# A gated-delta branch whose odd tile is multiplied first, with its norms moved and two memsets on GpSimd

## The chip, the cores and the metric

The kernel runs on one core of a Trainium2 chip. The metric is the device time of one execution in microseconds (us); a kernel's time is the median of several. Five engines work side by side and meet through semaphores: TensorE (PE, with PEld for its weight loads) multiplies, VectorE (DVE) and ScalarE (ACT) work element by element and can read TensorE's accumulator banks (`ps`), GpSimd (POOL) works element by element in on-chip memory, and SyncE (SP) issues the transfers (DMA). Each engine takes its own instructions strictly in order. An instruction that waits holds up all that stand behind it in its engine's queue.

## The reference, cut to what matters

The reference is a stack: a first block with two layers (three branches side by side in each: gated delta, latent attention, RWKV-7) and then a second block. The change lies in the gated-delta branch of the first block, so it is run twice. All is float32, one sequence of 1024 tokens with 1024 features.

```python
def gdn_branch(cols, conv_w, a_log, dt_bias, norm_g):   # cols = rms_norm(x) @ w_in, by columns
    qkv = jnp.concatenate([cols['gdn_q'], cols['gdn_k'], cols['gdn_v']], axis=-1)  # 384 + 384 + 384
    qkv = jax.nn.silu(centred_depthwise_conv(qkv, conv_w))                         # 5 taps in time
    q, k, v = jnp.split(qkv, [GDN_QK_W, 2 * GDN_QK_W], axis=-1)
    q = l2_normalize(q.reshape(b, l, GDN_HEADS, GDN_DK)) * (GDN_DK ** -0.5)
    k = l2_normalize(k.reshape(b, l, GDN_HEADS, GDN_DK))
    ...
    g = -jnp.exp(a_log) * jax.nn.softplus(a + dt_bias)
    beta = jax.nn.sigmoid(bt)
    o = gated_delta_chunked(...)                         # the next stage, in both directions
    o = rms_norm(bidir_merge(o), norm_g)
```

## The kernel before, in words

The stage is called `gdn_front` (lines 1488 to 1871 of the kernel before). It computes q, k and v up to the recurrence: 1152 columns, cut into nine tiles of 128. Feature-major, each tile is a matrix of 128 columns by 1024 tokens: tiles 0 to 2 are q, 3 to 5 are k, 6 to 8 are v. `hT` is the normed input, transposed.

For each tile n: multiply (TensorE), put the result into a padded buffer (`x_pad_g`, called `xp`), five taps of the convolution on VectorE in two halves of the tokens (`taps(n, b)`: one TENSOR_SCALAR and four SCALAR_TENSOR_TENSOR), and `silu` of each half on ScalarE into `gq`. The first six tiles (`NORMED`) are normed too: squares on GpSimd (`sq_g`), their sums by a matmul with a block matrix (`square_sums(n)`), `Ln` and `Exp` on ScalarE (`inverse_norm(n)`, into `rs_g`), and a product on VectorE (`normed(n)`). ScalarE has to load a table ahead of a function of another kind (ACT_TABLE_LOAD).

Eight of the nine tiles are multiplied in four pairs. A pair is a product of 2 by 2 blocks, done with seven block products in place of eight: P1 to P7, each four matmuls. Its inputs are the combinations T1 to T4 of blocks of `hT` (`combos_g`, once for the stage) and the sums S1 to S4 of blocks of the weights (`sums_g`, once for each pair). P1, P6, P7 and P4 add up one after the other in one bank of `ps`, and after each of the first three ScalarE copies the bank (`keep(1..3, j)` into `kept_g`), so each next one waits for that copy. P2 has a bank of its own; P5 and P3 add up in another. Three of the four result blocks are put together by VectorE (`block_of`: c11, c22, c12), the fourth (c21) is copied by ScalarE after P4 (`last_block`). The ninth tile is multiplied whole, in two halves of eight matmuls (`whole(b)`).

Pair j is tiles 2j and 2j+1, and the whole tile is number 8, last. The order on every engine is the one in which the code is written, engine by engine; no scheduler changes it. A buffer of `xp`, `acc_g`, `sq_g`, `rs_g` holds two tiles, chosen by n % 2. Weights of tiles 0 to 2 have been loaded by the stage ahead; SP loads the rest as their slots come free. The next stage (`gdn_chunk`) begins behind a barrier of all engines.

Of the kernel before, what the change touches and what calls it, by code (L numbers as in the profile page):

```python
# [25 lines left out]
ALU = mybir.AluOpType  # L26
# [110 lines left out]
def build(nc, io, values):  # L137
    with ExitStack() as ctx:
# [97 lines left out]
        for L in range(DEPTH):  # L236
# [1251 lines left out]
            with ExitStack() as st:  # L1488
# [11 lines left out]
                with ExitStack() as st2, nc.Block() as block:  # L1500
# [13 lines left out]
                    NP, WHOLE = 4, 8  # L1514
# [11 lines left out]
                    def left(j, r, k):  # L1526
                        return slot(2 * j + r)[:, 4 * k:4 * k + 4, :]
# [10 lines left out]
                    def inside(r, b):  # L1538
                        return xp[:, r, 2 + b * 512:2 + (b + 1) * 512]

                    def ready(n, b):
                        if n == WHOLE:
                            return ACT[f"whole_{b}"]
                        j, r = n // 2, n % 2
                        return ACT[f"c21_{j}"] if (r, b) == (1, 0) else VEC[f"c{r + 1}{b + 1}_{j}"]

                    @block.sync
                    def _(sp):
                        def columns(n):
                            sp.dma_start(slot(n), w_rows(w_in[:, COL_GDN + n * P:COL_GDN + (n + 1) * P])).then_inc(*DMA(f"w{n}"))  # L1550

                        columns(3)
                        sp.dma_start(tm_ab[:, :, :], tm_hbm[:, 0:2 * G2].rearrange("(t p) n -> p t n", p=P)).then_inc(*DMA("ab"))
                        for j in range(2, NP):
                            sp.wait_ge(*PE[f"P4_{j - 2}"])
                            sp.wait_ge(*VEC[f"S4_{j - 2}"])
                            columns(2 * j)
                            columns(2 * j + 1)
                        sp.wait_ge(*PE[f"P4_{NP - 2}"])
                        sp.wait_ge(*VEC[f"S4_{NP - 2}"])  # L1560
                        columns(WHOLE)

                    @block.tensor
                    def _(pe):
# [5 lines left out]
                        def first(j):  # L1570
                            if j >= 1:
                                pe.wait_ge(*DMA[f"w{2 * j}"] if j > 1 else DMA["w3"])
                            if j >= 2:
                                pe.wait_ge(*ACT[f"c21_{j - 2}"])
                            product("P1", j, chain_bank(j), left(j, 0, 0), right(0, 0))

                        def second(j):
                            if j:
                                pe.wait_ge(*VEC[f"c11_{j - 1}"])
                            product("P2", j, B_BANK, left(j, 0, 1), right(1, 0))  # L1580
# [20 lines left out]
                        def fifth(j):  # L1601
                            if j:
                                pe.wait_ge(*VEC[f"c12_{j - 1}"])
                            product("P5", j, D_BANK, sm[:, j % 2, 0], T[:, 0])

                        def fourth(j):
                            if j == 0:
                                pe.wait_ge(*VEC["T4"])
                            if j > 1:
                                pe.wait_ge(*DMA[f"w{2 * j + 1}"])  # L1610
                            pe.wait_ge(*ACT[f"s3_{j}"])
                            product("P4", j, chain_bank(j), left(j, 1, 1), T[:, 3], start=False)

                        def whole(b):
                            if b == 0:
                                pe.wait_ge(*DMA[f"w{WHOLE}"])
                                pe.wait_ge(*ACT[f"c21_{NP - 2}"])
                            else:
                                pe.wait_ge(*VEC[f"c11_{NP - 1}"])
                            for k in range(KD):  # L1620
                                q = pe.matmul(ps[:, (chain_bank(NP), B_BANK)[b], :], lhsT=slot(WHOLE)[:, k, :], rhs=hT[:, k, P + b * 512:P + (b + 1) * 512],
                                              start=(k == 0), stop=(k == KD - 1))
                            q.then_inc(*PE(f"whole_{b}"))
# [18 lines left out]

                        first(0)
                        second(0)
                        sixth(0)
                        fifth(0)
                        seventh(0)
                        gate_sums()
                        fourth(0)
                        for j in range(1, NP):  # L1650
                            first(j)
                            third(j - 1)
                            sixth(j)
                            second(j)
                            seventh(j)
                            fifth(j)
                            fourth(j)
                            square_sums(2 * j - 2)
                            square_sums(2 * j - 1)
                        whole(0)  # L1660
                        third(NP - 1)
                        whole(1)

                    @block.scalar
                    def _(act):
# [6 lines left out]
                        def last_block(j):  # L1672
                            act.wait_ge(*PE[f"P4_{j}"])
                            if j:
                                act.wait_ge(*VEC[f"tap{2 * j - 1}_1_{LAST}"])
                            act.copy(inside(1, 0), ps[:, chain_bank(j), :]).then_inc(*ACT(f"c21_{j}"))

                        def whole(b):
                            act.wait_ge(*PE[f"whole_{b}"])
                            act.wait_ge(*VEC[f"tap{WHOLE - 2}_1_{LAST}"])  # L1680
                            act.copy(inside(0, b), ps[:, (chain_bank(NP), B_BANK)[b], :]).then_inc(*ACT(f"whole_{b}"))
# [34 lines left out]

                        keep(1, 0)
                        gates()
                        keep(2, 0)
                        keep(3, 0)  # L1720
                        last_block(0)
                        gate_ends()
                        for j in range(1, NP):
                            keep(1, j)
                            silu(2 * j - 2, 0)
                            silu(2 * j - 1, 0)
                            silu(2 * j - 1, 1)
                            keep(2, j)
                            silu(2 * j - 2, 1)
                            keep(3, j)  # L1730
                            last_block(j)
                            inverse_norm(2 * j - 2)
                            inverse_norm(2 * j - 1)
                        silu(2 * NP - 2, 0)
                        silu(2 * NP - 1, 0)
                        silu(2 * NP - 1, 1)
                        silu(2 * NP - 2, 1)
                        whole(0)
                        whole(1)
                        silu(WHOLE, 0)  # L1740
                        silu(WHOLE, 1)

                    @block.vector
                    def _(vec):
# [10 lines left out]
                        def sums_of_left(j, which):  # L1755
                            a11, a12, a21, a22 = (left(j, r, k) for r, k in ((0, 0), (0, 1), (1, 0), (1, 1)))
                            if which == 0:
                                for n in (2 * j, 2 * j + 1):
                                    if n > 2:
                                        vec.wait_ge(*DMA[f"w{n}"])  # L1760
# [11 lines left out]
                        def block_of(j, r, b):  # L1772
# [3 lines left out]
                            vec.tensor_tensor(inside(r, b), kept[:, n - 1, :], ps[:, bank, :], ALU.add).then_inc(*VEC(f"c{r + 1}{b + 1}_{j}"))  # L1776
# [20 lines left out]
                        def cleared():  # L1797
                            vec.memset(G[:, :, :, :], 0.0).then_inc(*VEC("G"))
                            vec.memset(S[:, :, :, :], 0.0).then_inc(*VEC("S"))

# [18 lines left out]

                        combos_open()  # L1820
                        sums_of_left(0, 0)
                        sums_of_left(0, 1)
                        gates()
                        combos_close()
                        gate_rates()
                        block_of(0, 0, 0)
                        cleared()
                        taps(0, 0)
# [3 lines left out]
                        taps(1, 0)  # L1832
                        block_of(0, 0, 1)
                        taps(1, 1)
                        for j in range(1, NP):
                            taps(2 * j - 2, 1)
                            block_of(j, 0, 0)
                            taps(2 * j, 0)
                            if j == 1:
                                vec.wait_ge(*ACT["beta"])  # L1840
                                vec.wait_ge(*ACT["ends1"])
                                vec.tensor_tensor(kdw[:, :, :], kdw[:, :, :], gb[:, :, 1, :], ALU.mult).then_inc(*VEC("kdw"))
                            else:
                                normed(2 * j - 4)
                                normed(2 * j - 3)
# [4 lines left out]
                            taps(2 * j + 1, 0)  # L1850
                            block_of(j, 0, 1)
                            taps(2 * j + 1, 1)
                        taps(2 * NP - 2, 1)
                        normed(NORMED - 2)
                        normed(NORMED - 1)
                        taps(WHOLE, 0)
                        taps(WHOLE, 1)

                    @block.gpsimd
                    def _(pool):  # L1860
                        pool.memset(Y64[:, :, :, :], 0.0).then_inc(*POOL("Y64"))
                        for n in range(NORMED):
# [2548 lines left out]
```

## Time and profile before

| what | us |
|---|---|
| median of 3 runs (3723.2 to 3729.97) | 3729.53 |
| the profiled execution, its own time | 3734.25 |
| its span, first to last instruction | 3732.2 |
| `gdn_front`, first layer: 391.98 to 528.62 | 136.64 |
| `gdn_front`, second layer: 1518.43 to 1655.06 | 136.63 |
| PE busy in the first of them | 123.58 |
| DVE busy in it | 106.75 |
| ACT busy in it | 61.01 |
| POOL busy in it | 18.37 |

Times in the trace count from the start of the span. A row of the timeline gives start, duration, engine, line, operation, output<-inputs and count; in brackets the idle time of the engine ahead of it and what ended it. Instructions of one line that follow each other are merged, and the end of a product of matmuls is modelled: its 3.60 us overlap the next one by 0.17. Each float32 matmul shows as two. In the second layer the buffers are the same with `_again` behind their names.

### The profile page before, as it was taken

The page shows a single profiled execution, that of the slowest core. Times are in us where ns is not written, and L with a number is a line of the kernel's source. Part 1 is how long each engine was busy: PE and PEld are TensorE (multiplying, and loading weights), DVE is VectorE, ACT ScalarE, POOL GpSimd, SP SyncE. Part 2 cuts the span into 40 slices and gives each one's busy share as a digit, 9 for nine tenths or more (in the row PEclk, how much of TensorE's full clock was granted, in tenths as well). Part 3 has the DMA queues.
Part 4 walks back from the last instruction along what each step waited for, and adds up shares of the span by engine and source line. Part 5 has one row for each costly group of instructions (what it writes and reads, how often), then busy time and mean ns, then how long its engine had stood idle before and what let it go on. Part 6 is the DMA issues. An engine that isn't in the chain of part 4 may idle for free. (4 is left out here: it accounts for less than half of the span.)

```text
span 3732.2 us, 65872 instructions
## 1 busy us (share of the span) xinstructions
PE 3451.9 (92%) x27864; PEld 2104.2 (56%) x27864; DVE 2325.3 (62%) x4083; ACT 1221.8 (33%) x2143; POOL 290.5 (8%) x233
## 2 busy tenths in 40 slices
PE   7888879989999879988989988999999997999999
PEld 4367436666644467436766644666666664444444
DVE  3586778876653487678876653467766667433453
ACT  3353354535431254354534432122212121321002
POOL 0010100000000011100000000222222220000000
PEclk9899999999999999999999998999999998999999
DMA  4334212220053333312220042111111102213221
GB/s 164 104 92 131 67 34 85 81 101 12 13 187 113 99 90 111 93 34 85 80 103 12 10 156 82 35 41 45 46 41 46 40 24 87 86 42 112 90 96 45
DMA packets 302164, 281.51 MB, mean 75 GB/s; under 512 B 18208, under 2 KB 274592, under 8 KB 301872
## 3 DMA queue, kind: packets, MB, share of 16 engines
q1 hardware_dynamic: 301872, 277.30, 23.1%
q8 instruction: 222, 3.64, 0.4%
q14 instruction: 70, 0.57, 0.0%
HBM read 203.93 MB, written 73.33 MB: 74 GB/s over the span
## 5 line engine op out<-in xcount | busy, mean ns | idle before, releaser
L3716 DVE SCALAR_TENSOR_TENSOR cv<-glu,params,cv 128x1024 f32<-128x1024 f32 x240 | 361.0, 1504 | 6.4
L413 PE MATMUL ps<-hT,w_cols 128*128 128x512 f32 x448 | 198.9, 602 | 1.6 <-PEq L160 1.6
L4012 PE MATMUL ps<-hT,wr 128*128 128x512 f32 x360 | 161.7, 592 | 0.0
L413 PEld LDWEIGHTS ps<-hT,w_cols 128*128 128x128 f32 x448 | 85.2, 192 | 111.3 <-issue 111.2
L3692 POOL TENSOR_TENSOR Sp<-Sp,Rp 128x520 f32<-128x520 f32 (+1 forms) x56 | 88.5, 1581 | 566.2 <-DVE W L3733 566.2
L3475 PE MATMUL ps<-hT,w_f 128*128 128x347 f32 x384 | 116.3, 462 | 6.1 <-DMA w_f<-in_w_in 6.1
L3490 PE MATMUL ps<-w_i,hT 128*128 128x128 f32 x1024 | 120.7, 277 | 0.0
L3490 PEld LDWEIGHTS ps<-w_i,hT 128*128 128x128 f32 x1024 | 116.1, 192 | 2.2 <-issue 1.6
L4012 PEld LDWEIGHTS ps<-hT,wr 128*128 128x128 f32 x360 | 68.4, 190 | 86.1 <-issue 86.1
L3329 PE MATMUL ps<-w_out_again,mT_again 128*128 128x512 f32 x256 | 115.8, 612 | 0.0
L3475 PE MATMUL ps<-hT,w_glu_a 128*128 128x347 f32 x384 | 114.2, 456 | 0.4 <-ACT sgb L3656 0.4
L3482 PE MATMUL ps<-hT,w_g 128*128 128x512 f32 x256 | 114.1, 599 | 0.0
L3329 PE MATMUL ps<-w_out,mT 128*128 128x512 f32 x256 | 113.9, 604 | 0.0
L3475 PE MATMUL ps<-hT,w_glu_b 128*128 128x347 f32 x384 | 113.4, 454 | 0.0
L3482 PE MATMUL ps<-hT,w_q 128*128 128x512 f32 x256 | 111.2, 592 | 0.0
L4012 PE MATMUL ps<-combos_even,sums_of_w 128*128 128x512 f32 x240 | 107.9, 592 | 0.0
L3475 PEld LDWEIGHTS ps<-hT,w_f 128*128 128x128 f32 x384 | 72.9, 192 | 45.8 <-DMA w_f<-in_w_in 6.5
L1972 PE MATMUL ps<-fw_again,fh_again 128*128 128x384 f32 x256 | 91.2, 519 | 6.7 <-DVE AT_again L2368 3.5
L4098 ACT COPY kept_sums<-ps 128x512 f32<-128x512 f32 x46 | 27.0, 586 | 210.5 <-PE ps L4012 210.3
L3695 POOL TENSOR_TENSOR Rp<-Rp 128x520 f32<-128x520 f32 (+1 forms) x56 | 94.3, 1683 | 4.4
L2836 PE MATMUL ps<-kT_again,qT_again 96*128 96x512 f32 x192 | 92.5, 605 | 1.8 <-PEq L160 1.8
L2836 PE MATMUL ps<-kT,qT 96*128 96x512 f32 x192 | 92.5, 605 | 1.8 <-PEq L160 1.8
(975 smaller groups left out, 7350.9 us busy)
## 6 DMA issues: line engine op xcount, KB each, us to landing
w_cols<-in_w_in SPq DMA_DIRECT2D x30, 512.0 KB, 4.2
wr<-in_w_in SPq DMA_DIRECT2D x24, 512.0 KB, 5.2
hT_hbm<-hT SPq DMA_DIRECT2D x2, 4096.0 KB, 14.0
hT<-hT_hbm SPq DMA_DIRECT2D x2, 4096.0 KB, 15.9
fh<-hT_hbm SPq DMA_DIRECT2D x16, 512.0 KB, 4.7
fh_again<-hT_hbm SPq DMA_DIRECT2D x16, 512.0 KB, 4.6
x<-in_x SPq DMA_DIRECT2D x8, 512.0 KB, 9.0
ahead<-kb_hbm SPq DMA_DIRECT2D x16, 256.0 KB, 3.3
```

The costliest lines, as they stand in the source:

```text
L413: q = pe.matmul(ps[:, proj_bank(n, b), :], lhsT=wc[:, n % 3, k, :], rhs=hT[:, k, P + b * 512:P + (b + 1) * 512], start=(k == 0), stop=(k = ...
L1972: q = pe.matmul(ps[:, WB + n % 2, 0:FILL], lhsT=fh[:, n % 2, k, :], rhs=fw[:, k, :], start=(k == 0), stop=(k == KD - 1))
L2836: q = pe.matmul(ps[:, SCORES + 2 * (j % 2) + b, :], lhsT=qT[:, h, t * P:(t + 1) * P], rhs=kT[:, h, b * 512:(b + 1) * 512], start=True, sto ...
L3329: q = pe.matmul(ps[:, sum_bank(t, b), :], lhsT=mT[:, t % 2, k, :], rhs=wo[:, k, 512 * b:512 * (b + 1)], start=(k == 0), stop=(k == KD - 1))
L3475: q = pe.matmul(ps[:, BANK_X + b, 0:LONG], lhsT=wt[n][:, k, :], rhs=hT[:, k, T0 + b * LONG:T0 + (b + 1) * LONG], start=(k == 0), stop=(k = ...
L3482: q = pe.matmul(ps[:, bank + b, :], lhsT=wt[n][:, k, :], rhs=hT[:, k, P + b * 512:P + (b + 1) * 512], start=(k == 0), stop=(k == KD - 1))
L3490: q = pe.matmul(ps[:, BANK_X + b, (t % 3) * P:(t % 3 + 1) * P], lhsT=hT[:, k, t * P:(t + 1) * P], rhs=wt["i"][:, k, :], start=(k == 0), st ...
L3692: pool.tensor_tensor(S4[:, :, 0, :], S4[:, :, 0, :], R4[:, :, 1, (1 << k) - 1:1 << k].broadcast_to([P, n, 1 << k]), ALU.mult).then_inc(*PO ...
L3695: pool.tensor_tensor(R4[:, :, 1, :], R4[:, :, 1, :], R4[:, :, 0, (1 << k) - 1:1 << k].broadcast_to([P, n, 1 << k]), ALU.mult).then_inc(*PO ...
L3716: vec.scalar_tensor_tensor(out=cv[:, h % 2, :], in0=src, scalar=w, in1=cv[:, h % 2, :], op0=ALU.mult, op1=ALU.add).then_inc(*VEC(f"tap{h}_ ...
L4012: q = pe.matmul(ps[:, to, :], lhsT=a[:, k, :], rhs=b[:, k, :], start=(start and k == 0), stop=(k == 3), skip_group_check=True)
L4098: act.copy(sn[:, n // 2, :], ps[:, bank(j, "a"), :]).then_inc(*ACT(f"s{n}_{j}"))
```

## The change

The whole tile becomes tile 0 and is multiplied first, into the banks of P2 and P5; pair j is now tiles 2j+1 and 2j+2. Pair 0 runs P1, P6, P2, P7, P5, P4, where it ran P1, P2, P6, P5, P7, P4. The sums of squares of tile 2j-1 stand ahead of P4 of pair j, those of tile 2j behind it. `normed(2j-2)` and `normed(2j-1)` are done in pair j, where `normed(2j-4)` and `normed(2j-3)` were. The gates' first part stands at the head of VectorE's queue, and the memsets of `G` and `S` go from VectorE to GpSimd.

The diff, without three hunks that only renumber tiles:

```diff
-NP, WHOLE = 4, 8
+NP, WHOLE = 4, 0
...
 def left(j, r, k):
-    return slot(2 * j + r)[:, 4 * k:4 * k + 4, :]
+    return slot(2 * j + 1 + r)[:, 4 * k:4 * k + 4, :]
...
 def sum_bank(n, b):
...
-def inside(r, b):
-    return xp[:, r, 2 + b * 512:2 + (b + 1) * 512]
+def inside(n, b):
+    return xp[:, n % 2, 2 + b * 512:2 + (b + 1) * 512]
...
 def ready(n, b):
...
-    j, r = n // 2, n % 2
+    j, r = (n - 1) // 2, (n - 1) % 2
...
+    sp.wait_ge(*PE["whole_1"])
+    columns(4)
     for j in range(2, NP):
...
-        columns(2 * j)
...
-    sp.wait_ge(*PE[f"P4_{NP - 2}"])
-    sp.wait_ge(*VEC[f"S4_{NP - 2}"])
-    columns(WHOLE)
+        columns(2 * j + 2)
...
     def second(j):
...
+        else:
+            pe.wait_ge(*ACT["whole_0"])
...
     def fifth(j):
...
+        else:
+            pe.wait_ge(*ACT["whole_1"])
...
     def fourth(j):
...
-        if j > 1:
-            pe.wait_ge(*DMA[f"w{2 * j + 1}"])
+        if j:
+            pe.wait_ge(*DMA[f"w{2 * j + 2}"])
...
     def whole(b):
-        if b == 0:
-            pe.wait_ge(*DMA[f"w{WHOLE}"])
-            pe.wait_ge(*ACT[f"c21_{NP - 2}"])
-        else:
-            pe.wait_ge(*VEC[f"c11_{NP - 1}"])
         for k in range(KD):
-            q = pe.matmul(ps[:, (chain_bank(NP), B_BANK)[b], :], lhsT=slot(WHOLE)[:, k, :], rhs=hT[:, k, P + b * 512:P + (b + 1) * 512],
+            q = pe.matmul(ps[:, (B_BANK, D_BANK)[b], :], lhsT=slot(WHOLE)[:, k, :], rhs=hT[:, k, P + b * 512:P + (b + 1) * 512],
...
             pe.matmul(ps[:, sum_bank(n, b), :], lhsT=blk, rhs=sq[:, n % 2, half(b)], start=True,
                       stop=True).then_inc(*PE(f"sumsq{n}_{b}"))
 
+    whole(0)
+    whole(1)
     first(0)
+    sixth(0)
     second(0)
-    sixth(0)
-    fifth(0)
     seventh(0)
     gate_sums()
+    fifth(0)
     fourth(0)
+    square_sums(0)
...
         second(j)
         seventh(j)
         fifth(j)
+        square_sums(2 * j - 1)
         fourth(j)
-        square_sums(2 * j - 2)
-        square_sums(2 * j - 1)
-    whole(0)
+        if 2 * j < NORMED:
+            square_sums(2 * j)
     third(NP - 1)
-    whole(1)
...
     def last_block(j):
...
-        if j:
-            act.wait_ge(*VEC[f"tap{2 * j - 1}_1_{LAST}"])
-        act.copy(inside(1, 0), ps[:, chain_bank(j), :]).then_inc(*ACT(f"c21_{j}"))
+        act.wait_ge(*VEC[f"tap{2 * j}_1_{LAST}"])
+        act.copy(inside(2 * j + 2, 0), ps[:, chain_bank(j), :]).then_inc(*ACT(f"c21_{j}"))
...
     def whole(b):
...
-        act.wait_ge(*VEC[f"tap{WHOLE - 2}_1_{LAST}"])
-        act.copy(inside(0, b), ps[:, (chain_bank(NP), B_BANK)[b], :]).then_inc(*ACT(f"whole_{b}"))
+        act.copy(inside(WHOLE, b), ps[:, (B_BANK, D_BANK)[b], :]).then_inc(*ACT(f"whole_{b}"))
...
                 q = act.activation(to, whole, FN.Exp)
             q.then_inc(*ACT(f"ends{e}"))
 
+    whole(0)
+    whole(1)
     keep(1, 0)
     gates()
     keep(2, 0)
+    silu(WHOLE, 0)
+    silu(WHOLE, 1)
     keep(3, 0)
+    gate_ends()
     last_block(0)
-    gate_ends()
+    inverse_norm(0)
     for j in range(1, NP):
         keep(1, j)
-        silu(2 * j - 2, 0)
         silu(2 * j - 1, 0)
+        silu(2 * j, 0)
+        keep(2, j)
+        silu(2 * j, 1)
         silu(2 * j - 1, 1)
-        keep(2, j)
-        silu(2 * j - 2, 1)
         keep(3, j)
         last_block(j)
-        inverse_norm(2 * j - 2)
         inverse_norm(2 * j - 1)
-    silu(2 * NP - 2, 0)
-    silu(2 * NP - 1, 0)
-    silu(2 * NP - 1, 1)
-    silu(2 * NP - 2, 1)
-    whole(0)
-    whole(1)
-    silu(WHOLE, 0)
-    silu(WHOLE, 1)
+        if 2 * j < NORMED:
+            inverse_norm(2 * j)
+    for n, b in ((2 * NP - 1, 0), (2 * NP, 0), (2 * NP, 1), (2 * NP - 1, 1)):
+        silu(n, b)
...
-
-    def cleared():
-        vec.memset(G[:, :, :, :], 0.0).then_inc(*VEC("G"))
-        vec.memset(S[:, :, :, :], 0.0).then_inc(*VEC("S"))
...
         vec.wait_ge(*ACT[f"rs{n}"])
         vec.tensor_tensor(gq[:, n, :], gq[:, n, :], rs[:, n % 2, :], ALU.mult).then_inc(*VEC(f"normed{n}"))
 
+    gates()
     combos_open()
     sums_of_left(0, 0)
+    taps(WHOLE, 0)
     sums_of_left(0, 1)
-    gates()
     combos_close()
+    taps(WHOLE, 1)
     gate_rates()
     block_of(0, 0, 0)
-    cleared()
-    taps(0, 0)
+    taps(1, 0)
     sums_of_left(1, 0)
     sums_of_left(1, 1)
     block_of(0, 1, 1)
-    taps(1, 0)
+    taps(2, 0)
+    taps(2, 1)
+    vec.wait_ge(*ACT["beta"])
+    vec.wait_ge(*ACT["ends1"])
+    vec.tensor_tensor(kdw[:, :, :], kdw[:, :, :], gb[:, :, 1, :], ALU.mult).then_inc(*VEC("kdw"))
     block_of(0, 0, 1)
     taps(1, 1)
     for j in range(1, NP):
-        taps(2 * j - 2, 1)
+        normed(2 * j - 2)
         block_of(j, 0, 0)
-        taps(2 * j, 0)
-        if j == 1:
-            vec.wait_ge(*ACT["beta"])
-            vec.wait_ge(*ACT["ends1"])
-            vec.tensor_tensor(kdw[:, :, :], kdw[:, :, :], gb[:, :, 1, :], ALU.mult).then_inc(*VEC("kdw"))
-        else:
-            normed(2 * j - 4)
-            normed(2 * j - 3)
+        taps(2 * j + 1, 0)
         if j + 1 < NP:
             sums_of_left(j + 1, 0)
             sums_of_left(j + 1, 1)
         block_of(j, 1, 1)
-        taps(2 * j + 1, 0)
+        normed(2 * j - 1)
+        taps(2 * j + 2, 0)
+        taps(2 * j + 2, 1)
         block_of(j, 0, 1)
         taps(2 * j + 1, 1)
-    taps(2 * NP - 2, 1)
-    normed(NORMED - 2)
-    normed(NORMED - 1)
-    taps(WHOLE, 0)
-    taps(WHOLE, 1)
 
 @block.gpsimd
 def _(pool):
     pool.memset(Y64[:, :, :, :], 0.0).then_inc(*POOL("Y64"))
+    pool.memset(G[:, :, :, :], 0.0).then_inc(*POOL("G"))
+    pool.memset(S[:, :, :, :], 0.0).then_inc(*POOL("S"))
```

TensorE, between P4 of pair 1 and P6 of pair 2. `combos_g,w_cols` is P4 or P7, `sq_g` the sums of squares, `hT,w_cols` P1 or P2, `hT,sums_g` P3, `combos_g,sums_g` P6 or P5. Before:

```order
L1567 MATMUL ps<-combos_g,sums_g 128x512 x4
L1567 MATMUL ps<-combos_g,w_cols 128x512 x4
L1640 MATMUL ps<-sq_g,consts 128x512 x4
L1567 MATMUL ps<-hT,w_cols 128x512 x4
L1567 MATMUL ps<-hT,sums_g 128x512 x4
L1567 MATMUL ps<-combos_g,sums_g 128x512 x4
```

and after:

```order
L1566 MATMUL ps<-combos_g,sums_g 128x512 x4
L1638 MATMUL ps<-sq_g,consts 128x512 x2
L1566 MATMUL ps<-combos_g,w_cols 128x512 x4
L1638 MATMUL ps<-sq_g,consts 128x512 x2
L1566 MATMUL ps<-hT,w_cols 128x512 x4
L1566 MATMUL ps<-hT,sums_g 128x512 x4
L1566 MATMUL ps<-combos_g,sums_g 128x512 x4
```

Two of the four matmuls of the squares' sums went ahead of P4.

ScalarE at the same place, from the third copy of a pair to the first of the next (`rs_g` is `inverse_norm`), after the change:

```order
L1670 COPY kept_g<-ps 128x512
L1675 COPY x_pad_g<-ps 128x512
L1691 ACT_TABLE_LOAD
L1691 ACTIVATE rs_g<-ps,consts 128x512 x2
L1693 ACT_TABLE_LOAD
L1693 ACTIVATE rs_g<-rs_g 128x1024
L1691 ACT_TABLE_LOAD
L1691 ACTIVATE rs_g<-ps,consts 128x512 x2
L1693 ACT_TABLE_LOAD
L1693 ACTIVATE rs_g<-rs_g 128x1024
L1670 COPY kept_g<-ps 128x512
```

It is the same row for row as before, with other line numbers; only the tiles of the two norms are others.

VectorE at the end of the stage (`x_pad_g<-kept_g` is `block_of`, `gq<-gq,rs_g` is `normed`, 510 and 514 are the first and second half of a tile's taps). Before:

```order
L1776 TENSOR_TENSOR x_pad_g<-kept_g,ps 128x512
L1810 TENSOR_SCALAR acc_g<-x_pad_g,params 128x514
L1813 SCALAR_TENSOR_TENSOR acc_g<-x_pad_g,params,acc_g 128x514 x4
L1810 TENSOR_SCALAR acc_g<-x_pad_g,params 128x514
L1813 SCALAR_TENSOR_TENSOR acc_g<-x_pad_g,params,acc_g 128x514 x4
L1818 TENSOR_TENSOR gq<-gq,rs_g 128x1024 x2
L1810 TENSOR_SCALAR acc_g<-x_pad_g,params 128x510
L1813 SCALAR_TENSOR_TENSOR acc_g<-x_pad_g,params,acc_g 128x510 x4
L1810 TENSOR_SCALAR acc_g<-x_pad_g,params 128x514
L1813 SCALAR_TENSOR_TENSOR acc_g<-x_pad_g,params,acc_g 128x514 x4
```

and after:

```order
L1774 TENSOR_TENSOR x_pad_g<-kept_g,ps 128x512
L1812 TENSOR_TENSOR gq<-gq,rs_g 128x1024
L1804 TENSOR_SCALAR acc_g<-x_pad_g,params 128x510
L1807 SCALAR_TENSOR_TENSOR acc_g<-x_pad_g,params,acc_g 128x510 x4
L1804 TENSOR_SCALAR acc_g<-x_pad_g,params 128x514
L1807 SCALAR_TENSOR_TENSOR acc_g<-x_pad_g,params,acc_g 128x514 x4
L1774 TENSOR_TENSOR x_pad_g<-kept_g,ps 128x512
L1804 TENSOR_SCALAR acc_g<-x_pad_g,params 128x514
L1807 SCALAR_TENSOR_TENSOR acc_g<-x_pad_g,params,acc_g 128x514 x4
```

Before, the last `block_of` (c12 of pair 3) is followed by four sets of taps and two norm products; after, by one set of taps, and a norm product stands ahead of both sets of taps of tile 8.

## Rows read from the trace of the kernel before

**Rows 1.** The page, part 1: an engine's busy time, share of the span, instructions.

```profile
PE 3451.9 (92%) x27864; PEld 2104.2 (56%) x27864; DVE 2325.3 (62%) x4083; ACT 1221.8 (33%) x2143; POOL 290.5 (8%) x233
```

**Rows 2.** Windows, both copies of the stage: length, each engine's busy time, clock, DMA.

```profile
391.98:528.62 136.64, 123.58 (x288) 54.48 (x288) 106.75 (x138) 61.01 (x83) 18.37 (x13) 0.96 0.10 24
1518.43:1655.06 136.63, 123.58 (x288) 54.53 (x288) 106.76 (x138) 61.02 (x83) 18.36 (x13) 0.96 0.10 24
```

**Rows 3.** Timeline of PE: start, duration, what, count [idle before, releaser].

```profile
391.98 8.80 PE L1567 MATMUL ps<-hT,w_cols 128*128 128x512 f32 x16 [4.41 <-PEq L160]
400.62 7.03 PE L1567 MATMUL ps<-combos_g,sums_g 128*128 128x512 f32 x16
...
410.92 0.99 PE L1629 MATMUL ps<-gb,consts 128*128 128x48 f32 x8
...
435.96 3.60 PE L1567 MATMUL ps<-combos_g,w_cols 128*128 128x512 f32 x8
...
450.69 3.67 PE L1567 MATMUL ps<-combos_g,sums_g 128*128 128x512 f32 x8 [0.84 <-DVE x_pad_g L1776]
...
479.53 3.67 PE L1567 MATMUL ps<-combos_g,sums_g 128*128 128x512 f32 x8 [1.14 <-ACT kept_g L1670]
...
493.34 3.60 PE L1567 MATMUL ps<-combos_g,w_cols 128*128 128x512 f32 x8
```

**Rows 4.** Timeline of ACT, between two pairs and at the end.

```profile
439.59 0.59 ACT L1676 COPY x_pad_g<-ps 128x512 f32<-128x512 f32 x1 [6.28 <-PE ps L1567]
440.20 1.28 ACT L1693 ACT_TABLE_LOAD   x1
441.49 1.26 ACT L1693 ACTIVATE rs_g<-ps,consts 128x512 f32<-128x512 f32 x2
442.77 1.28 ACT L1695 ACT_TABLE_LOAD   x1
444.07 1.06 ACT L1695 ACTIVATE rs_g<-rs_g 128x1024 f32<-128x1024 f32 x1
...
449.98 0.57 ACT L1670 COPY kept_g<-ps 128x512 f32<-128x512 f32 x1
...
527.99 0.63 ACT L1686 ACTIVATE gq<-acc_g 128x514 f32<-128x514 f32 x1 [2.93 <-DVE acc_g L1813]
```

**Rows 5.** Timeline of DVE in the first copy of the stage.

```profile
399.54 2.29 DVE L1751 TENSOR_TENSOR combos_g<-hT 128x2048 f32<-128x2048 f32 x1
...
405.70 1.76 DVE L1798 MEMSET G_g<- 128x2048 f32 x1 [0.38 <-issue]
407.57 0.70 DVE L1799 MEMSET S_g<- 128x768 f32 x1
...
431.45 5.74 DVE L1813 SCALAR_TENSOR_TENSOR acc_g<-x_pad_g,params,acc_g 128x510 f32<-128x510 f32 x4
...
510.78 0.69 DVE L1776 TENSOR_TENSOR x_pad_g<-kept_g,ps 128x512 f32<-128x512 f32 x1 [9.55 <-PE ps L1567]
...
518.50 2.35 DVE L1818 TENSOR_TENSOR gq<-gq,rs_g 128x1024 f32<-128x1024 f32 x2
520.77 0.48 DVE L1810 TENSOR_SCALAR acc_g<-x_pad_g,params 128x510 f32<-128x510 f32 x1
...
524.31 0.48 DVE L1810 TENSOR_SCALAR acc_g<-x_pad_g,params 128x514 f32<-128x514 f32 x1
```

**Rows 6.** Timeline of POOL, its first two rows in the stage.

```profile
391.95 2.66 POOL L1861 MEMSET Y_g<- 128x3072 f32 x1 [22.39 <-POOLq L160]
431.11 5.53 POOL L1868 TENSOR_TENSOR sq_g<-gq 128x512 f32<-128x512 f32 x4 [36.50 <-ACT gq L1686]
```

**Rows 7.** DMA issues from 392.3: count, KB each, us to landing.

```profile
tm_ab<-tm_hbm SPq DMA_DIRECT2D x1, 96.0 KB, 4.0
```

**Rows 8.** Windows after a rest of 3.46 us, next stage (columns of rows 2).

```profile
563.60:567.00 3.40, 3.38 (x6) 1.89 (x7) 3.25 (x6) 3.28 (x8) 0.00 (x0) 0.50 0.00 0
567.00:571.00 4.00, 4.00 (x10) 2.26 (x9) 4.00 (x24) 0.38 (x1) 0.00 (x0) 0.68 0.00 0
```

More of the change, by code:

```diff
@@ L1571, in first @@
                             if j >= 1:
-                                pe.wait_ge(*DMA[f"w{2 * j}"] if j > 1 else DMA["w3"])
+                                pe.wait_ge(*DMA[f"w{2 * j + 1}"])
                             if j >= 2:
@@ L1757, in sums_of_left @@
                             if which == 0:
-                                for n in (2 * j, 2 * j + 1):
+                                for n in (2 * j + 1, 2 * j + 2):
                                     if n > 2:
@@ L1775, in block_of @@
                             vec.wait_ge(*PE[f"{done}_{j}"])
-                            vec.tensor_tensor(inside(r, b), kept[:, n - 1, :], ps[:, bank, :], ALU.add).then_inc(*VEC(f"c{r + 1}{b + 1}_{j}"))
+                            vec.tensor_tensor(inside(2 * j + 1 + r, b), kept[:, n - 1, :], ps[:, bank, :], ALU.add).then_inc(*VEC(f"c{r + 1}{b + 1}_{j}"))
                         def gates():
```

## The prediction

> **What bounds the kernel now.** I read the page first. TensorE is busy for 92% of the span [rows 1], but that is an average over many stages. The change touches one stage only, so what counts is when that stage ends. The windows view shows the stage twice, once for each of the two layers of the first block (the second copy's buffers have `_again` in their names): 136.64 us and 136.63 us long, with the same work in both [rows 2]. Every step below is worked out on the first copy and the sum is doubled. The stage lies between two block ends that stop all engines, so nothing of the next stage starts before its last instruction: what the stage loses or gains goes to the total in full.
>
> Next, the timeline of TensorE [rows 3]. A product of four matmuls (eight rows of the trace, since each matmul is recorded twice) starts every 3.43 us (6.87 us for two: 400.62 to 407.49, the end of 7.03 less the 0.17 by which ends overlap). The first two took 8.64 us (391.98 to 400.62), 1.77 us more: in the window from the stage's start the engine comes from rest at the lower of its two clock levels (1.2 GHz, against 2.4 GHz later). There are just two idle times inside the stage, 0.84 us at 450.69 and 1.14 us at 479.53, both in front of the sixth product (`P6`) of a pair. The last P4 starts at 493.34.
>
> Then ScalarE [rows 4]. It copies the end of P4 (439.59), and then the two norms of the pair stand in its queue: for each a table load, two `Ln`, another table load and an `Exp`, 9.8 us for both without a gap. Only behind them stands the copy of the next pair's P1 (449.98), for which P6 waits: from the start of P4 (435.96) to the start of the next P6 (450.69) it is 14.73 us. At the stage's end VectorE works alone, from 510.78, when it gets the last product that it waits for, to the eighteenth `silu`, which ends at 528.62 [rows 4, 5].
>
> **The change part by part.** *Whole tile first.* Its two products of eight matmuls move from the end to the front. TensorE has 13.7 us more ahead of the pairs and none behind; VectorE gets its 7.2 us of taps on this tile early, where it waited for products. The extra weight load for tile 4 is issued once the whole tile is multiplied (about 408), 19 us before it is wanted and with nothing else in the queue: no cost.
>
> *Start of pair 0.* The order is now P1, P6, P2, P7. P6 adds into P1's bank and waits for ScalarE to have copied it. No product stands between, so the copy shows: 0.17 (the end of the modelled product) + 0.04 + 0.59 + 0.14, together 0.94 us. The trace has no such place; the nearest bounds are 0 and the 1.14 us of the stall at 479.53 [rows 3]. I take 0.94. A product behind a stall takes 0.07 us more (3.67 against 3.60).
>
> *Gates first on VectorE.* Its head now waits for the small load of gate columns, which lands 4.0 us after its issue at 392.4 [rows 7]. Queued behind it are the combinations T1, T2, the sums of left sides and everything after: 5 us later. P6 wants T2 and the first sums at 412, P7 wants T3 at 419. From 396.4 the gates take 0.5, T1 and T2 4.6 (2.29 us for such an instruction [rows 5]), two sums of left sides 1.3: 402.8. Then the whole tile's first taps 3.6, two more sums 1.3, T3 2.3: 410. Nothing on the path; bounds 0 and, if the load came 4 us later, still 0.
>
> *Two memsets.* 1.76 us plus 0.7 us leave VectorE [rows 5]. GpSimd takes them behind its memset of 2.66 us for 3072 elements [rows 6], 2816 elements or about 2.4 us, in a time when it has 36.5 us of rest. No cost and no gain, as VectorE waits there for P2.
>
> *Squares and norms.* Now one norm in pair 0, two in pairs 1 and 2, one in pair 3. In front of P6 of pairs 2 and 3 ScalarE still has two norms, so P6 can't start before P4 + 14.73 us, as now. But TensorE has only one tile's sums (1.72 us instead of 3.43) between P4 and P1: it arrives at 3.43 + 1.72 + 6.87 = 12.02 us. The stall is 2.71 us, twice. Before, the two gaps cost 1.00 and about 1.3 us (0.17 more than the idle shown). For pair 1 there is one norm (4.95 us) and no stall. The removed sums don't save time: they stand elsewhere in the pair (behind P5).
>
> *Norms in VectorE's queue.* `normed(2j-1)` now stands between the block `c22` and the taps of tile 2j+2, and its factor comes from a norm that ScalarE starts only after copying P4. VectorE waits until P4's start + 9.17 us (from 435.96 to the end of the first `Exp`, 445.13 [rows 3, 4]); behind it are queued both taps of tile 2j+2, c12 and the taps of tile 2j+1. In pairs 1 and 2 this is hidden: c12 is ready at P4 + 18.3 us, P7 wants it (through the second copy) at P4 + 21.6. In pair 3 nothing follows that could hide it, and it sets the end.
>
> The Trainium skill, *ScalarE: Activation LUTs*, section *What ACT_TABLE_LOAD costs*, gives 1283 ns for a load, as these rows have it, and 1380 ns of drain for each switch. The rows show no drain: a load of 1.28 us at 442.77 is followed by `Exp` at 444.07, and began 0.02 us after `Ln` [rows 4]. By the page the norms would take 2.8 us longer each and the stage some 14 us; I go by the rows.
>
> **The sum.** Start 391.98; whole tile 13.73 and slow clock 1.77; P1 3.43; stall 0.94; P6 3.51; P2, P7 6.87; gate sums 0.93 (0.99 less 0.06 of overlap [rows 3]); P5 3.51: P4 of pair 0 starts at 426.7. Pair 1: 12.02 + four products and a tile's sums, 15.44: 454.1. Pairs 2 and 3: 14.73 + 15.52 = 30.25 each (now 28.5 and 28.8): P4 of pair 3 starts at 514.6. From there: factor of tile 5 at 9.17, 0.03, `normed(5)` 1.14 (half of the step from 518.5 to 520.77), taps 3.54 (520.77 to 524.31) and about the same, 3.56, c12 0.60 (0.69 less the overlap), taps of tile 7 with the way to ScalarE 3.68 (524.31 to 527.99), `silu` 0.63 [rows 4, 5], together 22.4: 537.0 us. Now it is 528.62. That is 8.4 us more, and 16.7 us in both layers. Against 3734.25 us of the profiled run it makes 3751.0; the run lies 4.7 us above the median of 3729.53, and the predicted median is 3746.3 us.
>
> GpSimd slows VectorE when both read: four tap instructions took 5.74 us beside the squares at 431.11, where a whole set of five takes 3.54 [rows 5, 6]. After the change the squares of pairs 1 and 2 fall beside the first taps of tile 3 and 5, where it costs nothing: even with 6.2 us for these taps (P4 + 23.7 to 29.9), four left sums (2.6) and c22 (0.6), VectorE is at its held norm at P4 + 33.1, and the factor comes 9.2 us after the next P4, at P4 + 39.4. None fall in the tail. Bounds 0 and 2.6 us; I take 0.
>
> **The rivals.**
> 1. *VectorE isn't held at the end* (the factor of tile 5 is there in time, only the stalls act). Then the taps of tile 8 start after the copy of P4, at P4 + 4.25, and the stage ends at 530.9: +2.3, twice 4.6: 3734.1 us. Against it stands the code's own order on ScalarE, copy first and then norm.
> 2. *P6 stalls no longer than now, but VectorE is held.* 3.1 us less per layer: 3740.0 us.
> 3. *Neither: not slower.* The mechanism is a short norm chain on ScalarE, which decides below 1.7 us for the tail and below 12.0 us for P6. The stage would end 0.8 us earlier, 3727.9 us. Against it: eight steps without a gap in rows 4. The same page of the Trainium skill, section *Table sets: the hidden batching unit*, says that `Ln` and then `Exp` want one load, from a set with both; the rows show a load between them, and the same loads stand in the changed order.
> 4. *The clock falls in the new stalls.* After 3.46 us of rest TensorE ran at 0.50 of its clock for 3.4 us and 0.68 for the next 4.0 [rows 8], a loss of 3.0 us. The new stalls are shorter (2.71 and 0.94), and those of 0.84 and 1.14 us cost only 0.07. If all four longer ones fell: +12, 3758.3 us; one or two of them 3749 to 3752.
> 5. *The change isn't what it says.* That could only be if compiled queues had another order; they haven't.
>
> **How the numbers follow.** Forecast 0.70, rival 1 0.07, rival 2 0.05, rival 3 0.06, clock 0.12. 0.2% of this kernel is 7.5 us, about what a measurement can tell from no change. Forecast, rival 2 and the clock lie above it, less a little for scatter of the medians (the three runs shown spread over 6.8 us): slower 0.83. Rivals 1 and 3 are same, with that scatter: 0.14. Faster would need 7.5 us out of a stage whose gain in the best case is 1.6: 0.03. The forecast's own range is 3741 to 3751; with most of the clock case above, and down towards rival 1, 3737 to 3754.
>
> **What would show it.** In the changed profile: P4 of pair 3 starts at 514 to 515; two idle times of 2.5 to 2.9 us before P6 of pairs 2 and 3, with ScalarE's copy as the releaser; one of 0.8 to 0.9 us before the first P6; VectorE idle for about 10 us before the last `gq<-gq,rs_g`, with `Exp` as releaser; the stage 145.0 us long in both layers. It is wrong if that last wait is missing, if P6 doesn't stall, if the clock falls inside the stage, or if the first VectorE wait reaches P6 of pair 0.

## The result and the profile after

The changed kernel took 3741.05 us (median of 6 runs, 3738.95 to 3747.03) against 3729.3 us (6 runs): ratio 1.0036, 95% interval 1.0024 to 1.0049, so 13 us slower, between 9 and 18. The forecast of 3746.3 us lies 5 us too high; the median is inside the forecast's own range (3741 to 3751) by only 0.05 us. Slower was given 0.83.

The stage is longer in both layers. These windows of the changed kernel answer to [rows 2], with the same columns:

```profile
394.41:539.63 145.22, 123.86 (x288) 54.47 (x288) 102.02 (x136) 62.32 (x84) 19.11 (x15) 0.95 0.09 23
1526.99:1673.63 146.64, 125.27 (x288) 54.97 (x288) 101.83 (x136) 62.32 (x84) 18.93 (x15) 0.93 0.09 23
```

145.22 and 146.64 us, where it was 136.64 and 136.63: 8.6 and 10.0 us more. No engine has much more work. TensorE's timeline in the first copy (columns as in [rows 3]) shows where it rests:

```profile
394.41 15.82 PE L1619 MATMUL ps<-hT,w_cols 128*128 128x512 f32 x32 [4.22 <-PEq L160]
410.06 3.60 PE L1566 MATMUL ps<-hT,w_cols 128*128 128x512 f32 x8
414.43 3.67 PE L1566 MATMUL ps<-combos_g,sums_g 128*128 128x512 f32 x8 [0.77 <-DVE combos_g L1751]
...
456.60 3.60 PE L1566 MATMUL ps<-combos_g,w_cols 128*128 128x512 f32 x8
...
471.33 3.67 PE L1566 MATMUL ps<-combos_g,sums_g 128*128 128x512 f32 x8 [2.55 <-ACT kept_g L1670]
...
501.58 3.67 PE L1566 MATMUL ps<-combos_g,sums_g 128*128 128x512 f32 x8 [2.55 <-ACT kept_g L1670]
...
517.11 3.60 PE L1566 MATMUL ps<-combos_g,w_cols 128*128 128x512 f32 x8
```

From P4 (456.60) to the next P6 (471.33) it is 14.73 us, to the hundredth what [rows 3] had there. TensorE now comes to P6 1.7 us earlier, because two matmuls of the squares' sums are gone from between, and rests 2.55 us in place of 0.84 and 1.14. (The 0.77 us in the first pair is put down to VectorE's T4, which ends at 414.43, but P6 doesn't read T4: it waits for ScalarE's copy of P1, which in the second layer the profile names.) VectorE at the end of the first copy (columns as in [rows 5]):

```profile
515.66 0.69 DVE L1774 TENSOR_TENSOR x_pad_g<-kept_g,ps 128x512 f32<-128x512 f32 x1 [0.83 <-PE ps L1566]
526.31 1.23 DVE L1812 TENSOR_TENSOR gq<-gq,rs_g 128x1024 f32<-128x1024 f32 x1 [9.96 <-ACT rs_g L1693]
527.45 0.48 DVE L1804 TENSOR_SCALAR acc_g<-x_pad_g,params 128x510 f32<-128x510 f32 x1
```

It rests for 9.96 us in front of `normed(5)`, while the block that the taps behind it need was copied at 521.33. Both waits have the same source, ScalarE's queue behind P4 of the last pair:

```profile
520.74 0.59 ACT L1675 COPY x_pad_g<-ps 128x512 f32<-128x512 f32 x1 [8.00 <-PE ps L1566]
521.35 1.28 ACT L1691 ACT_TABLE_LOAD   x1
522.64 1.27 ACT L1691 ACTIVATE rs_g<-ps,consts 128x512 f32<-128x512 f32 x2
523.93 1.28 ACT L1693 ACT_TABLE_LOAD   x1
525.22 1.06 ACT L1693 ACTIVATE rs_g<-rs_g 128x1024 f32<-128x1024 f32 x1
```

The sums for this norm were done at 517.3, as P4 began (517.11). The stage began at 394.41 in place of 391.98, so P4 of pair 3 stands at 517.11 and not at the 514 to 515 of the prediction; counted from the stage's start it is 122.7 us, where the sum had 122.6.

The extra 1.4 us of the second copy come from the clock. Windows of the changed kernel, P6 of pair 3 in the first and in the second copy:

```profile
501.60:505.10 3.50, 3.50 (x9) 1.59 (x10) 3.30 (x6) 2.29 (x3) 0.00 (x0) 1.00 0.00 0
1634.00:1639.10 5.10, 5.09 (x9) 2.26 (x10) 4.83 (x8) 2.32 (x3) 0.00 (x0) 0.69 0.00 0
```

After the same rest of 2.55 us the same product ran at 1.00 of the clock the first time, and at 0.69 the second.

### The profile page after: what moved, and what is told of

It is laid out like the page before. It is cut to its first block and busy times, and to the rows that moved or that the text cites. A ratio compares the mean times of both kernels' runs of the same rounds, so it can differ in the third digit from the quotient of the medians.

```text
span 3745.2 us, 65872 instructions
## 1 busy us (share of the span) xinstructions
PE 3452.1 (92%) x27864; PEld 2104.7 (56%) x27864; DVE 2315.5 (62%) x4079; ACT 1224.5 (33%) x2145; POOL 291.3 (8%) x237
## 5 line engine op out<-in xcount | busy, mean ns | idle before, releaser
L1963 PE MATMUL ps<-fw,fh 128*128 128x384 f32 x256 | 91.1, 517 | 4.0 <-DVE AT L2359 3.5
```

Of the source, the lines that this page charges most:

```text
L1963: q = pe.matmul(ps[:, WB + n % 2, 0:FILL], lhsT=fh[:, n % 2, k, :], rhs=fw[:, k, :], start=(k == 0), stop=(k == KD - 1))
```

## The experiments

Theory A is the forecast's: ScalarE's queue of norms behind P4 sets P6 and the end of the stage, and no other part of the change matters. Ratios are against the kernel before, measured in the same job; the first five rows and the last four are two jobs, in which the kernel before had medians of 3726.5 us (27 runs) and 3726.0 us (22 runs). Where stage lengths are compared, they are from one profiled execution of each kernel, first and second copy.

| kernel | stage, us | rest before P6 of pairs 2 and 3, us | VectorE held before `normed(5)`, us | ratio (95%) |
|---|---|---|---|---|
| before | 136.6, 136.6 | 0.84, 1.14 | none | 1 |
| changed, again | 145.1, 148.0 | 2.55, 2.55 | 9.95 | 1.0044 (1.0031 to 1.0058) |
| normed(5) last | 141.7, 139.4 | 2.55, 2.55 | none | 1.0017 (1.0009 to 1.0026) |
| norms apart | 141.1, 139.7 | none | 8.2 | 1.0010 (1.0001 to 1.0018) |
| norm before the copy | 134.4, 135.5 | none | 5.1 | 0.9986 (0.9978 to 0.9995) |
| one load for two | 142.1, 142.4 | none | 8.2 | 1.0031 (1.0019 to 1.0042) |
| gates, memsets back | 147.6, 147.6 | 2.55, 2.55 | 9.96 | 1.0046 (1.0032 to 1.0059) |
| norm first, P2 between | 133.4, 133.8 | none | 5.1 | 0.9985 (0.9977 to 0.9994) |
| before, one load for two | 134.2, 134.2 | none | none | 0.9989 (0.9981 to 0.9998) |

**The changed kernel again.** No edit.

> The changed kernel once more, to measure the whole against the sum of its stage. Theory A (the loss is the norm queue on ScalarE: two stalls before P6, and VectorE held at the end): each copy of the stage is 145.2 us long instead of 136.6, and the whole is 17 us slower than before, ratio 1.0046, unless something outside the stage gives some of it back. Theory B (part of it is really given back outside the stage, which the first profile suggested with 4 us): the ratio is again about 1.0035 and the stages between the two copies are again 2 to 4 us shorter than before. If the 4 us were scatter, these stages come out as long as before or longer.

The ratio was 1.0044, which is 16 us (12 to 22). The stage was 145.06 and 147.99 us long; in the second copy the clock fell once more, and TensorE began more slowly. The stages between the two copies took 992.8 us (535.41 to 1528.16) where in the kernel before they took 989.8 and in the first profile of the changed kernel 987.4. The differences have both signs, so no gain outside the stage is shown.

Both profiled executions of the changed kernel were the slowest of their groups (3747.03 us, median 3741.05; 3749.92 us, median 3743.85), and at 0.967 and 0.966 their granted clock over the whole run was at the low end (the others reach 0.969 and 0.970). So their stages, 18.6 and 19.8 us longer in the two layers together, may be somewhat longer than those of a middle execution.

**normed(5) last.**

```diff
                             block_of(j, 1, 1)
-                            normed(2 * j - 1)
+                            if j < NP - 1:
+                                normed(2 * j - 1)
...
                             taps(2 * j + 1, 1)
+                        normed(NORMED - 1)
```

> The changed kernel with only normed(5) put behind the last taps on VectorE (it was in front of the taps of tile 8). Theory A: the taps of tile 8 start as soon as P4 is copied, P4 + 4.3 us in place of P4 + 10.4; the stage ends at P4 of pair 3 + 16.9 in place of 22.5, so it is 139.6 us long and the whole 11 us faster than the changed kernel, about 3734 us by a before of 3729. The two stalls before P6 stay at 2.55. Rival (VectorE's amount of work and not its order sets the end): the norm product and the taps fill the same time, and the end moves by less than 2 us per layer.

The second copy was 139.41 us long, as theory A had it. The first was 2.3 us longer for the clock alone (slower start, and P6 of pair 3 in 5.16 us in place of 3.67). VectorE at the end of the second copy of this kernel:

```profile
1644.48 0.69 DVE L1774 TENSOR_TENSOR x_pad_g_again<-kept_g_again,ps 128x512 f32<-128x512 f32 x1 [0.83 <-PE ps L1566]
1650.18 0.49 DVE L1804 TENSOR_SCALAR acc_g_again<-x_pad_g_again,params 128x510 f32<-128x510 f32 x1 [5.01 <-ACT x_pad_g_again L1675]
```

The taps start with the copy of P4, and the order on VectorE, not its work, was worth 5.6 us a layer (145.06 less 139.41, less 0.05 of slow start).

**Norms apart.**

```diff
                             keep(1, j)
+                            if j > 1:
+                                inverse_norm(2 * j - 2)
                             silu(2 * j - 1, 0)
...
                             inverse_norm(2 * j - 1)
-                            if 2 * j < NORMED:
-                                inverse_norm(2 * j)
```

> The changed kernel with the second norm of a pair put behind the first copy of the next pair on ScalarE, nothing else. Theory A: ScalarE copies P1 at P4 + 9.2 us, P6 does not wait, the two idle times of 2.55 us go to below 0.2, the stage is 5.6 us shorter (139.6 us) and the whole 11 us faster than the changed kernel. VectorE is still held for 10 us before the last normed. Rival (P6 is late for VectorE's sums or for the weights): the idle times stay.

Both rests of 2.55 us are gone. Second copy 139.70 us, first 141.10 with a slower start (its first 32 rows took 17.02 us against 15.62). TensorE, P1, P3 and P6 of pair 2 in this kernel:

```profile
459.20 3.60 PE L1566 MATMUL ps<-hT,w_cols 128*128 128x512 f32 x8
462.64 3.60 PE L1566 MATMUL ps<-hT,sums_g 128*128 128x512 f32 x8
466.07 3.60 PE L1566 MATMUL ps<-combos_g,sums_g 128*128 128x512 f32 x8
```

VectorE was held for 8.2 us and not for the 10 us that I expected: `normed(5)` started at P4 + 9.20 as before, but VectorE came to it 1.7 us later, counted from P4.

The two losses are separate in place and nearly equal in size, 5.6 and 5.4 us a layer.

**Norm before the copy.**

```diff
                             keep(3, j)
-                            last_block(j)
                             inverse_norm(2 * j - 1)
+                            last_block(j)
```

> The changed kernel with one line moved on ScalarE: the norm of tile 2j-1 in front of the copy of P4, not behind it (its sums are there before P4 starts). Theory A says that both losses hang on this place: the factor is ready at P4 + 5.1 us in place of 9.2, the copy of P4 at P4 + 5.8 in place of 4.2, the next pair's P1 is copied at P4 + 11.2 in place of 14.6 and P6 is not late (12.0). No stall before P6, the stage about 10.6 us shorter, 134.7 us long, the whole 21 us faster than the changed kernel and 4 us faster than before. Rival (the two losses have two causes): only one of them goes, 5 to 6 us per layer. Rival (the whole tile at the front costs in itself): the stage stays longer than the 136.6 us of before.

134.41 and 135.46 us: one moved line takes away nearly all of both losses. The medians say the same: changed 3743.9 us, `normed(5)` last 3733.9, norms apart 3731.9, norm before the copy 3722.3. That is 10.0, 12.0 and 21.6 us less, so the two losses add up. ScalarE in pair 2 of this kernel (P4 starts at 453.24):

```profile
452.58 0.69 ACT L1691 ACTIVATE rs_g<-ps,consts 128x512 f32<-128x512 f32 x1 [2.41 <-PE ps L1638]
453.44 0.69 ACT L1691 ACTIVATE rs_g<-ps,consts 128x512 f32<-128x512 f32 x1 [0.17 <-PE ps L1638]
454.14 1.28 ACT L1693 ACT_TABLE_LOAD   x1
455.44 1.06 ACT L1693 ACTIVATE rs_g<-rs_g 128x1024 f32<-128x1024 f32 x1
456.87 0.59 ACT L1675 COPY x_pad_g<-ps 128x512 f32<-128x512 f32 x1 [0.38 <-PE ps L1566]
...
462.61 0.57 ACT L1670 COPY kept_g<-ps 128x512 f32<-128x512 f32 x1
```

The first norm of pair 2 fits wholly beside P4: its table load went into an earlier wait, and its `Exp` ends at 456.50. The copy of P4 isn't even late (P4 + 3.63 us, as before), where I had expected it 1.6 us later, and the copy of P1 begins at P4 + 9.4 us. In pair 3 it is otherwise. Its P4 starts at 508.17, the load had not gone ahead, and ScalarE copies P4 only behind the `Exp`, with VectorE still held:

```profile
512.39 0.57 ACT L1675 COPY x_pad_g<-ps 128x512 f32<-128x512 f32 x1
512.52 1.23 DVE L1812 TENSOR_TENSOR gq<-gq,rs_g 128x1024 f32<-128x1024 f32 x1 [5.10 <-ACT rs_g L1693]
```

The copy is 0.6 us late there, and the taps start behind the norm product, at P4 + 5.5 us; with `normed(5)` last they started at P4 + 4.3. So about 1.2 us a layer of the second loss are left. The stage is nevertheless shorter than the 136.6 us of before: the whole tile at the front doesn't make it longer, once this is right.

**One load for two.**

```diff
-                            inverse_norm(2 * j - 1)
-                            if 2 * j < NORMED:
-                                inverse_norm(2 * j)
+                            inverse_norms(*([2 * j - 1, 2 * j] if 2 * j < NORMED else [2 * j - 1]))
```

`inverse_norms` runs every `Ln` of its tiles and then every `Exp`.

> The changed kernel with the two norms of a pair computed together on ScalarE: four Ln, then two Exp, so two table loads in place of four; same arithmetic. Theory A with a load at 1.28 us and nothing behind it: the next copy of P1 comes 2.6 us earlier, the stalls before P6 fall from 2.55 to about 0.1. But the first factor of the pair is ready 1.2 us later, VectorE's c12 with it, and P7 now waits about 1.1 us for the second copy, which waits for c12. Stage 3.3 us shorter (141.9 us), the whole 6 to 7 us faster than the changed kernel. Rival (a switch of tables costs 2.66 us with its drain): the saving is over 5 us before P6, no more than the stall itself, and the load rows would be followed by a gap. Rival (VectorE's held order has no reach into TensorE): no wait before P7, stage 5 us shorter.

The stall before P6 is gone, and a new one stands before P7, as expected. The whole is 7.2 us below the next version, which was measured in the same job and has all the stalls (3738.0 against 3745.1 us; 6 to 7 expected). TensorE and then ScalarE, pair 2:

```profile
464.06 3.60 PE L1566 MATMUL ps<-combos_g,sums_g 128*128 128x512 f32 x8
467.49 3.60 PE L1566 MATMUL ps<-hT,w_cols 128*128 128x512 f32 x8
472.14 3.67 PE L1566 MATMUL ps<-combos_g,w_cols 128*128 128x512 f32 x8 [1.05 <-ACT kept_g L1670]
```

```profile
457.57 2.42 ACT L1701 ACTIVATE rs_g<-ps,consts 128x512 f32<-128x512 f32 x4
460.01 1.28 ACT L1704 ACT_TABLE_LOAD   x1
461.31 2.00 ACT L1704 ACTIVATE rs_g<-rs_g 128x1024 f32<-128x1024 f32 x2
463.21 0.56 ACT L1670 COPY kept_g<-ps 128x512 f32<-128x512 f32 x1
...
471.41 0.59 ACT L1670 COPY kept_g<-ps 128x512 f32<-128x512 f32 x1 [3.58 <-DVE x_pad_g L1783]
```

The second copy (471.41) waits for VectorE's c12, which stands behind the held `normed`. So that order reaches into TensorE as soon as P6 is no longer late. The load of 1.28 us begins 0.02 us after `Ln` and `Exp` begins 0.02 us after it: no drain.

**Gates and memsets back.**

```diff
-                        gates()
                         combos_open()
                         sums_of_left(0, 0)
+                        gates()
...
                         block_of(0, 0, 0)
+                        vec.memset(G[:, :, :, :], 0.0).then_inc(*VEC("G"))
+                        vec.memset(S[:, :, :, :], 0.0).then_inc(*VEC("S"))
```

and both memsets off GpSimd.

> The changed kernel with two parts undone: the gates' first part stands behind the first sums of left sides on VectorE again, and the two memsets are back on VectorE, behind the first block of pair 0. Theory A: nothing changes beyond 0.3 us per layer, since P6 of pair 0 waits for the copy of P1 and P7 for a combination that is ready early; the idle before the first P6 stays 0.8 us. Rival (VectorE's wait of 4.3 us for the gate columns at its head is on the path): the stage gets 1 to 4 us shorter. Rival (the memsets on GpSimd gain): it gets 2.5 us longer.

The ratio is that of the changed kernel. Both copies are 147.6 us long, 2.4 us more than 145.2, which looks like the 2.5 us of the rival that has the memsets gain on GpSimd. The rows put it elsewhere. P6 after a stall took 5.26 and 5.25 us once in each copy (1.6 us), and the first P6 came 20.84 us after the stage's start against 20.02, with the same idle of 0.77 us before it: in the first 5 us the granted clock was 0.50 here and 0.63 in the first profile of the changed kernel. The rest is 145.2. No cost or gain of either part shows.

**Norm first, P2 between.** The moved norm, and for pair 0:

```diff
                         first(0)
-                        sixth(0)
                         second(0)
+                        sixth(0)
+                        fifth(0)
                         seventh(0)
                         gate_sums()
-                        fifth(0)
                         fourth(0)
```

> The changed kernel with the norm of tile 2j-1 in front of the copy of P4 on ScalarE, and pair 0's products in the order of before (P1, P2, P6, P5, P7, P4). Theory A: no idle time of TensorE in the stage at all; P4 of pair 3 starts 121 us after the stage's start and the stage is 133.8 us long, 0.9 us less per layer than with the moved norm alone. The whole about 6 us below before, 3723 us by a before of 3729. Rival (TensorE loses something else at the start, such as the clock): the first pair is not shorter by 0.9.

No idle time of TensorE is left in the stage; 133.43 and 133.75 us. P4 of pair 3 starts 115.8 us after the stage's start (505.50 less 389.74), not 121 as I had expected; that figure doesn't fit the expected stage either, since 17.7 us follow it. The whole, 3721.9 us against 3726.0 (11 and 22 runs), is below the kernel before by its interval, but can't be told from the moved norm alone, whose 3722.3 us is the same; the 0.9 us per layer are seen in the trace only (the stage's difference less that of the slow start).

**Before, one load for two.** The same `inverse_norms(2 * j - 2, 2 * j - 1)` in the kernel before.

> The kernel before, with only the two norms of a pair computed together on ScalarE (two table loads in place of four). Theory A: the copy of P1 comes 2.6 us earlier, both idle times before P6 (0.84 and 1.14) go, the stage is 2.3 to 2.8 us shorter (134 us) and the whole 5 us faster than before: the queue of norms on ScalarE was already TensorE's only wait before the change. Rival (the end of this stage hangs on VectorE's queue and not on P6): no change of the time though the idle times go.

134.18 and 134.19 us, both rests gone: the norms on ScalarE held TensorE already before the change. The whole is 3.8 us faster, where I had expected 5. This version and the last can't be told apart (3722.2 and 3721.9 us). The best version here with the whole tile first is 0.4 to 0.8 us a layer shorter than this one; as the two have different repairs on ScalarE, no run shows how much of that is the whole tile's.

## Why the prediction was right

*Whole tile first.* No cost shows, as the stage with the moved norm is below that of before. The weight load was in time. No run has the whole tile first alone.

*Start of pair 0.* 0.94 us expected; idle 0.77 and 0.17 of overlap, so 0.94.

*Gates and memsets.* At nothing, and nothing it was, though VectorE waited 4.34 us for the gate columns.

*Squares and norms.* 2.71 us of stall expected; the trace has 2.55 and the 0.17 of overlap, in all eight stalls of the two profiled executions of the changed kernel. Taking these away alone gave 5.4 us a layer.

*Norms in VectorE's queue.* The factor at P4 + 9.17: 526.28 less 517.11 is 9.17. Taking the wait away gave 5.6 us a layer. The stage was forecast at 145.0 us and the first copy is 145.2.

*GpSimd beside VectorE.* Hidden, as worked out: VectorE rested 8.70 and 7.04 us before the two earlier held norms.

*The clock.* This is what the prediction had wrong. Of the 16 stalls of 2.55 us in four profiled executions (the changed kernel twice, `normed(5)` last, gates and memsets back) five were followed by a P6 of 5.16 to 5.26 us, one or two in each execution. So the condition of rival 4, which had 0.12, was met each time, and with it one of the prediction's own signs of being wrong, that the clock falls inside the stage. What kept this small is the price: 1.5 to 1.6 us each and not the 3.0 that [rows 8] gave for a rest of 3.46 us. That is 0.5 us per stall on average, 2 us in the whole, which the sum lacked.

The slow start was sized too small as well. The sum took 1.77 us from the first 16 rows of before (8.80 us); over the 16 copies that begin with the whole tile the 32 rows took 16.05 us on average, which is 2.15 us of slow clock, 0.4 us more a layer. The kernel before and its one-load version had 8.80 us in all four of their copies; whether the order does that or chance, no run shows.

*The whole.* The stages of the first profile grew by 18.6 us and its span by 13.0. Most of the rest is in the profile of before: from the second copy's end to the end of the span it has 2077.1 us (3732.2 less 1655.06), while all nine other executions have 2070.6 to 2073.7, the changed kernel 2071.6. The sum was made on an execution that happened to be long by 3.4 to 6.5 us in a part that the change doesn't touch; its difference of 16.7 us stands within both measured intervals. The second job gave 17.3 us between the medians (3743.85 and 3726.51), the first 11.8. Two measurements of the same kernel lie 5.5 us apart, so the medians can't judge terms of 2 us, and that the first fell inside the narrow range is partly luck. What bears the forecast out is the rows: both waits at the place and in the size that it gave.

Rivals 1, 2 and 3 fell: none of the waits was missing. Rival 3's short chain was made in experiments, by taking one of the two norms out of it or two of its four loads. Its price was wrong: it had the stage 0.8 us shorter than before, but with P6 free at P4 + 12.0 the rests that stood there before go too. By the prediction's own rows that is 3.1 us shorter a layer, 133.5 us; with the moved norm the first copy came to 134.4, with 1.2 us of the hold left in it. The best case that the chance of faster was set against is so 6 us and not 1.6, still under the 7.5 us that it would have needed.

Two statements of the Trainium skill, *ScalarE: Activation LUTs*, did not hold here. It adds about 1380 ns of drain to each load (section *What ACT_TABLE_LOAD costs*); in the version with one load for two the load begins 0.02 us after the `Ln` ahead of it, and the `Exp` 0.02 us after the load. It has one load serve `Ln` and then `Exp` (section *Table sets: the hidden batching unit*); here a load stands between them, four for two norms. Its advice to do all of one set before switching (section *Rules for kernel authors*) did hold: it took the rests before P6 away in two kernels, 2.55 us twice in one (where 1.05 us came up before P7) and 0.84 and 1.14 us in the other.

## What to carry to other kernels

When work is taken out from between two uses of a bank, ask what the next use waits for: here it was the copy at the end of another engine's queue, and TensorE only came to the same wait earlier. In an in-order queue put first what is ready first: the norm whose sums were there before P4, and not the copy that had to wait for P4. A consumer that is moved up in its queue gains nothing, or holds up all behind it, if its producer isn't moved up too.

## What the runs showed of the hardware

After equal rests of 2.55 us TensorE came back at a granted clock of 1.00 eleven times in sixteen, and five times it ran the next product at 0.69 or 0.70 on average; after rests of 0.77 us (14 times) and 1.05 us (4 times) it was never slow. At the stage's start, after rests of 3.92 to 4.42 us, the whole tile's 32 rows took between 15.35 and 17.04 us (16 copies), so a stage that begins at the low clock varied by 1.7 us from one execution to the next.
